# Sums of weight blocks moved from Pool to DVE, and joint DVE instructions, in the up projection of a hybrid decoder layer

## The reference, cut to what matters

```python
def conv_gated_mlp(h, w_up, ffn_conv, w_down):
    u = causal_dwconv(h @ w_up, ffn_conv)      # (1024, 1024) @ (1024, 5632), 3 taps along positions
    gate, up = jnp.split(u, 2, axis=-1)
    return (jax.nn.silu(gate) * up) @ w_down   # (1024, 2816) @ (2816, 1024)
```

## Time and profile before

| | |
|---|---|
| Median of 3 runs | 1482.48 us (1482.26 to 1483.81) |
| The profiled execution's own time | 1481.3 us |
| Its span in the profile | 1479.6 us |
| PE busy | 1433.3 us, 97% |
| DVE busy | 1056.7 us, 71% |
| ACT busy | 702.7 us, 47% |
| Pool busy | 367.9 us, 25% |
| Mean granted clock of TensorE | 0.993 |
| Pairs of the up projection | about 779 to 1130 us of the span |
| Down projection | about 1130 to 1352 us |

### The profile page before, as it was taken

How to read it: one execution, slowest core, us unless ns; L and a number is a source line. 1 busy time by engine, 2 the same in 40 slices (tenths; PEclk the granted TensorE clock), 3 DMA queues, 4 the chain that set the end, 5 groups by cost and what they waited for, 6 DMA issues and landing times.

```text
span 1479.6 us, 19630 instructions
## 1 busy us (share of the span) xinstructions
PE 1433.3 (97%) x7167; PEld 1199.8 (81%) x7167; DVE 1056.7 (71%) x1467; ACT 702.7 (47%) x1297; POOL 367.9 (25%) x314
## 2 busy tenths in 40 slices
PE   6999999999989999999999999999999999999996
PEld 5777888878879999888888887887788886888885
DVE  6666545551038888367897999999999599577566
ACT  5432456412326877357664443443345444454434
POOL 3000001100028677010013333332330387010010
PEclk9999999999998999999999999999999999999999
DMA  8653424545522332544442333334327755424232
GB/s 220 78 105 43 43 69 125 154 96 120 143 78 72 115 108 82 183 144 156 138 145 87 100 125 133 113 104 152 115 85 267 225 170 178 143 79 129 86 99 100
DMA packets 156318, 181.52 MB, mean 123 GB/s; under 512 B 21240, under 2 KB 96190, under 8 KB 156222
## 3 DMA queue, kind: packets, MB, share of 16 engines
q1 hardware_dynamic: 155968, 180.16, 42.4%
q10 hardware_dynamic: 254, 0.10, 0.0%
HBM read 130.95 MB, written 49.28 MB: 122 GB/s over the span
## 4 chain that ended last, share of the span: by engine, by line
PE 81%; DVE 13%; issue 2%; ACT 2%; DMA 1%; POOL 0%; SPq 0%; DVEq 0%; ACTq 0%; POOLq 0%
PE psum L2255 7%; PE psum L2257 7%; PE psum L2256 7%; PE psum L563 5%; PE psum L565 5%; PE psum L564 5%; PE psum L1202 5%; PE psum L2167 4%; PE psum L2169 4%; PE psum L2168 4%; PE psum L2194 3%; PE psum L2195 3%; PE psum L2196 3%; PE psum L1256 3%; PE psum L618 3%; PE psum L620 3%
## 5 line engine op out<-in xcount | busy, mean ns | idle before, releaser
L148 DVE TENSOR_TENSOR w_wlo<-w_raw,w_whi 128x1024 fp32r<-128x1024 f32 x70 | 93.8, 1340 | 253.8 <-ACT w_whi L142 253.7
L2255 PE MATMUL psum<-m_hi,w_whi 128*128 128x512 f32 x416 | 163.0, 392 | 7.1 <-DVE w_wlo L1821 6.3
L2257 PE MATMUL psum<-m_hi,w_wlo 128*128 128x512 f32 x416 | 162.0, 389 | 0.0
L2256 PE MATMUL psum<-m_lo,w_whi 128*128 128x512 f32 x416 | 161.9, 389 | 0.0
L142 ACT ACTIVATE w_whi<-w_raw 128x1024 fp32r<-128x1024 f32 x70 | 74.0, 1058 | 184.2 <-PE psum L2169 85.7
L563 PE MATMUL psum<-h_hi,w_whi 128*128 128x512 f32 x320 | 126.6, 396 | 3.1 <-DVE h_lo L834 3.1
L565 PE MATMUL psum<-h_hi,w_wlo 128*128 128x512 f32 x320 | 125.2, 391 | 0.0
L564 PE MATMUL psum<-h_lo,w_whi 128*128 128x512 f32 x320 | 125.1, 391 | 0.0
L2194 PE MATMUL psum<-w_whi,g_slot 128*128 128x512 f32 x308 | 122.3, 397 | 2.7 <-DVE w_wlo L2969 2.4
L2195 PE MATMUL psum<-w_wlo,g_slot 128*128 128x512 f32 x308 | 121.2, 394 | 0.0
L2196 PE MATMUL psum<-w_whi,g_slot 128*128 128x512 f32 x308 | 121.2, 393 | 0.0
(11 more groups left out here) (377 smaller groups left out, 3656.8 us busy)
## 6 DMA issues: line engine op xcount, KB each, us to landing
w_raw<-in_w_up SPq DMA_DIRECT2D x39, 512.0 KB, 4.0
w_raw<-in_w_in SPq DMA_DIRECT2D x36, 512.0 KB, 6.5
s_rows<-formed_sums SPq DMA_DIRECT2D x11, 1024.0 KB, 4.1
w_raw<-s_rows SPq DMA_DIRECT2D x44, 256.0 KB, 2.7
g_rows<-long_g SPq DMA_DIRECT2D x18, 512.0 KB, 2.7
w_raw<-g_rows SPq DMA_DIRECT2D x33, 256.0 KB, 3.1
w_raw<-in_w_out SPq DMA_DIRECT2D x16, 512.0 KB, 4.3
mixed_home<-in_w_down SPq DMA_DIRECT2D x32, 256.0 KB, 3.5
```

Of the source, the lines that this page charges most:

```text
L2255: pe.matmul(out, wh[:, part], hi(kt), start=(start and kt == 0), stop=False)
L2256: pe.matmul(out, wh[:, part], lo(kt), start=False, stop=False)
L2257: ins = pe.matmul(out, wl[:, part], hi(kt), start=False, stop=(stop and kt == KT // 2 - 1))
```

## The change

It has four parts.

- The 72 sums of the pairs go from Pool to DVE. Those of pair 0 stand between pieces of `dve_plain` (T1 behind piece 29, T2 behind the second tap of unit 6, T3 behind piece 30, T4 behind piece 33). In `dve_pairs`, T1 of pair c+1 stands behind remainder n+5, T2 behind n+6, T3 behind n+7 and T4 behind n+9. Pool has nothing to do in the pairs.
- The two results of T3 become one instruction over 1024 elements: the PSUM bank is read twice through a broadcast, and both outputs lie at one distance in a common buffer, `work`.
- NS2 and S3 of nine of the eleven formed sets (those from the pairs' own gated values) become one instruction, `e0` read twice, at the place of NS2.
- The down projection's Pool sums come in another order and behind other waits: the second group is split, so that B12's sums come last, and each group waits for the remainder of piece 14+i, 25+i, 36+i and 47+i.

For the joint instructions the buffers of the pairs lie in one tile. `copies[0]` now lies where `h_raws` was, so ACT waits once, in pair 0, for the last remainder taken from there (`sum_lo`); `short_acc` of the last plain unit lies in `formed`. A gap grows from 16 to 24 elements.

```diff
-        gap = s("home_gap", [P, 16])
+        gap = s("home_gap", [P, 24])
...
+                work = s("pair_work", [P, 8 * HALF + 6 * SEQ + 8], c=pairs)
+                line_at, form_at = 4 * HALF, 4 * HALF + 2 * SEQ + 8
+                g_at, acc_at = form_at + 4 * HALF, form_at + 4 * HALF + 2 * SEQ
...
+        def both(at, step):
+            return work[:, at:at + 2 * step].rearrange("p (b c) -> p b c", b=2)[:, :, 0:HALF]
+        u_early = line_at + self.PAD
+        self.copies_12, self.copy_3_and_line = both(HALF, HALF), both(3 * HALF, u_early - 3 * HALF)
+        self.forms_12, self.form_0_and_e1 = both(form_at + HALF, HALF), both(form_at, g_at + HALF - form_at)
...
     def made_count(self, m, i):
-        n = self.KH
-        return {2: i + 1, 4: n + 2 * i + 1, 5: n + 2 * i + 2, 6: 3 * n + i + 1}[m]
+        return {2: 0, 4: 1, 6: 2, 5: 3}[m] * self.KH + i + 1
...
             m.wait(act, key)
+            if c == 0:
+                act.wait_ge(s["sum_lo"], 2 * KT)
...
         if which in (self.NS2, self.S4):
             dve.wait_ge(s["formed"], 4 * use + (1 if which == self.NS2 else 3))
+        if i >= Units.PLAIN // 2 and which == self.S3:
+            return
+        if i >= Units.PLAIN // 2 and which == self.NS2:
+            twice = e0.unsqueeze(1).broadcast_to([P, 2, HALF])
+            dve.tensor_tensor(self.forms_12, twice, self.form_0_and_e1, ALU.subtract).then_inc(s["formed"], 2)
+            return
...
         piece(29)
+        units.sum(dve, 0, Units.T1, self.s["gated"])
         taps(6, 0)
+        units.sum(dve, 0, Units.T2)
         piece(30)
+        units.sum(dve, 0, Units.T3)
...
         piece(33)
+        units.sum(dve, 0, Units.T4)
         gate(6)
...
             units.remainder(dve, n + 5)
+            if c == 0:
+                for stored in (base - 2, base - 1):
+                    self.g_stored(dve, stored)
+            units.sum(dve, c + 1, Units.T1)
...
             units.remainder(dve, n + 6)
+            units.sum(dve, c + 1, Units.T2)
...
             self.dve_rest(dve, n + 7)
+            units.sum(dve, c + 1, Units.T3)
...
-            dve.tensor_tensor(self.long_line[1][:, early], of(p7), copy[2], ALU.add)
-            self.banks.release(dve.tensor_tensor(copy[3], of(p7), copy[1], ALU.add), p7)
+            twice = of(p7).unsqueeze(1).broadcast_to([P, 2, HALF])
+            self.banks.release(dve.tensor_tensor(self.copy_3_and_line, twice, self.copies_12, ALU.add), p7)
...
             self.dve_rest(dve, n + 9)
+            units.sum(dve, c + 1, Units.T4)
             self.dve_form(dve, c, self.S4)
...
     def pool(self, pool):
-        units = self.units
         for i in range(0, self.HT, 2):
             self.add(pool, "outp0", i)
-        units.sum(pool, 0, Units.T1, self.s["gated"])
-        units.sum(pool, 0, Units.T2)
-        units.sum(pool, 0, Units.T3)
-        units.sum(pool, 0, Units.T4)
-        for c in range(Units.PAIRS):
-            if c == 0:
-                for n in (2 * Units.PLAIN - 2, 2 * Units.PLAIN - 1):
-                    self.g_stored(pool, n)
-            for which in (Units.T1, Units.T2, Units.T3):
-                units.sum(pool, c + 1, which)
-            units.sum(pool, c + 1, Units.T4)
         self.pool_down(pool)
...
-        made, split = self.s["down_made"], lambda m, i: self.units.ready(pool, self.piece(m * self.KH + i))
+        made, left = self.s["down_made"], lambda u: self.units.ready(pool, self.piece(u))
...
-            split(0, i)
+            left(self.KH + self.AHEAD + i)
             pool.tensor_tensor(home(self.B11), home(self.B12), home(self.B11), ALU.subtract).then_inc(made, 1)
...
-            split(2, i)
+            left(2 * self.KH + self.AHEAD + i)
             pool.tensor_tensor(home(self.B11), home(self.B11), home(self.B22), ALU.subtract).then_inc(made, 1)
-            pool.tensor_tensor(home(self.B12), home(self.B22), home(self.B12), ALU.subtract).then_inc(made, 1)
...
-            split(1, i)
+            left(3 * self.KH + self.AHEAD + i)
             pool.tensor_tensor(home(self.B21), home(self.B21), home(self.B11), ALU.add).then_inc(made, 1)
+        for i in range(self.KH):
+            left(4 * self.KH + self.AHEAD + i)
+            pool.tensor_tensor(home(self.B12), home(self.B22), home(self.B12), ALU.subtract).then_inc(made, 1)
```

More of the change, by code:

```diff
@@ L1881, in __init__ @@
             with ExitStack() as pairs:
[L1882 to L1888, removed]
+                work = s("pair_work", [P, 8 * HALF + 6 * SEQ + 8], c=pairs)
+                line_at, form_at = 4 * HALF, 4 * HALF + 2 * SEQ + 8
+                g_at, acc_at = form_at + 4 * HALF, form_at + 4 * HALF + 2 * SEQ
+                self.copies = [work[:, i * HALF:(i + 1) * HALF] for i in range(4)]
+                long = lambda at, n: [work[:, at + u * n:at + (u + 1) * n] for u in range(2)]
+                self.long_line, self.long_g, self.long_acc = long(line_at, self.PAD + SEQ), long(g_at, SEQ), long(acc_at, SEQ)
+                self.long_line.reverse()
+                formed = work[:, form_at:g_at].rearrange("p (w c) -> p w c", w=4)
+        def both(at, step):
[3 more added lines that the diff above has]
+        self.forms_12, self.form_0_and_e1 = both(form_at + HALF, HALF), both(form_at, g_at + HALF - form_at)
+        odd, last = [sums[0][:, u, :] for u in range(2)], [formed[:, u, :] for u in range(2)]
         self.short_acc = [([self.acc[0][:], self.acc[1][:]], odd)[n % 2] for n in range(2 * Units.PLAIN - 1)] + [last]
         self.short_g = [sums[1][:, part, :] for part in range(2)]
-        self.formed, self.formed_all = [formed[:, i, :] for i in range(4)], formed[:]
+        self.formed, self.formed_all = [formed[:, i, :] for i in range(4)], formed
         with ExitStack() as ple:
@@ L2051, in store_g @@
         else:
-            i, src, part = n - Units.PLAIN, self.long_g[:, n % 2, :], slice(0, SEQ)
+            i, src, part = n - Units.PLAIN, self.long_g[n % 2], slice(0, SEQ)
         sp.dma_start(self.g_rows[i, :, part], src).then_inc(self.g_out[n % 2], 16)
@@ L2573, in act_down @@
             if u == 1:
-                self.act_smooth(act, 2 * Units.PLAIN + last, self.long_acc[0][:], self.FREED + 2 * (2 * Units.PLAIN + last + 1))
+                self.act_smooth(act, 2 * Units.PLAIN + last, self.long_acc[0], self.FREED + 2 * (2 * Units.PLAIN + last + 1))
             if product in (0, 2) and 0 <= t < self.HT:
@@ L2637, in act_pairs @@
                 self.banks.released(act, ("pair", c - 1, Units.B21))
-            self.banks.release(act.activation(self.copies[0][:], self.banks.of(key), ACT.Copy), key)
+            self.banks.release(act.activation(self.copies[0], self.banks.of(key), ACT.Copy), key)
             units.round(act, n + 4)
@@ L2645, in act_pairs @@
             else:
[L2646 removed]
+                self.act_smooth(act, base + c - 1, self.long_acc[0], self.FREED + 2 * (base + c))
             units.round(act, n + 6)
@@ L2655, in act_tap_up @@
         act.wait_ge(self.s["gated"], 2 * Units.PLAIN + c)
-        act.activation(self.long_acc[1][:], self.long_line[1][:, 0:SEQ], ACT.Copy,
+        act.activation(self.long_acc[1], self.long_line[1][:, 0:SEQ], ACT.Copy,
                        scale=self.first_tap(2 * Units.PLAIN + c, 1)).then_inc(self.s["tap0"], 1)
@@ L2662, in act_tap_gate @@
         act.wait_ge(self.s["gated"], 2 * Units.PLAIN + c)
-        act.activation(self.long_acc[0][:], self.long_line[0][:, 0:SEQ], ACT.Copy,
+        act.activation(self.long_acc[0], self.long_line[0][:, 0:SEQ], ACT.Copy,
                        scale=self.first_tap(2 * Units.PLAIN + c, 0)).then_inc(self.s["tap0"], 1)
@@ L2951, in dve_gate @@
         else:
-            out, acc, used = self.long_g[:, n % 2, :], [tile[:] for tile in self.long_acc], n >= 2 * Units.PLAIN + 2
+            out, acc, used = self.long_g[n % 2], self.long_acc, n >= 2 * Units.PLAIN + 2
         if used:
@@ L2981, in dve_form @@
         else:
-            e0, e1 = (self.long_g[:, 0, part] for part in (slice(0, HALF), slice(HALF, SEQ)))
-            o0, o1 = (self.long_g[:, 1, part] for part in (slice(0, HALF), slice(HALF, SEQ)))
+            e0, e1 = (self.long_g[0][:, part] for part in (slice(0, HALF), slice(HALF, SEQ)))
+            o0, o1 = (self.long_g[1][:, part] for part in (slice(0, HALF), slice(HALF, SEQ)))
             if which == self.S1:
@@ L3148, in dve_pairs @@
         late = slice(self.PAD + HALF, self.PAD + SEQ)
-        early = slice(self.PAD, self.PAD + HALF)
-        of, copy = self.banks.of, [tile[:] for tile in self.copies]
+        of, copy = self.banks.of, self.copies
         for c in range(Units.PAIRS):
@@ L3154, in dve_pairs @@
                 self.dve_join(dve, c - 1, Units.T4)
-                self.dve_taps(dve, last, 0, self.long_acc[1][:], self.long_line[1], 1)
+                self.dve_taps(dve, last, 0, self.long_acc[1], self.long_line[1], 1)
             units.remainder(dve, n + 3)
@@ L3190, in dve_join @@
```

(14 more changed lines are left out.)

6 lines of the change are left out of this document (3 added, 3 removed).

## The result

| | before | after |
|---|---|---|
| Median of the runs | 1482.37 us (1480.94 to 1483.81, 4 runs) | 1465.26 us (1464.80 to 1466.26, 4 runs) |
| Ratio to before, 95% interval | | 0.9885 (0.9868 to 0.9903) |
| Profiled execution, own time and span | 1481.3 and 1479.6 us | 1465.5 and 1463.7 us |

The account below looks back on a forecast made before the run. PE was taken to set the time, with DVE, slowed beside Pool's sums, holding it up. Winning 7.7 us in the pairs and 4.6 in the down projection took 1482.48 to 1470.2 us, range 1468 to 1477.

Parts of the forecast that it names:

- 7.7 us were counted as lost: Pairs: PE's 123 pieces took 342.3 us against 334.6 without stalls; all 7.7 us were counted as won.
- the new sums' slot 0.60: Pairs: each sum moved to DVE takes 0.60 us, eight in two pairs adding 4.8 us of DVE work.
- the joint instructions 1.13 against 1.14: Pairs: a joint instruction takes DVE 1.14 us like the gate, against 2 x 0.60; three save 0.2 us in two pairs.
- no wait for landed tiles: Pairs: T1's sum on DVE finds its two tiles landed, as SP issues them about a pair earlier; counted at 0.
- the idle place filled: Pairs: DVE's idle 0.5 us per pair, ahead of the remainder that waits for ACT's rounding, is likely filled by T1's sum.
- the 36.2 counted: Pairs: DVE's work for two pairs after the change with the idle place filled, 36.2 us against PE's 38.1.
- the stretch: Pairs: Pool's sums lengthen DVE's instructions with two SBUF inputs, by 6.3 us in two pairs, which the change removes.
- the slower rival: Pairs: the stretch has another cause than Pool, so added sums remove nothing; +41 us, 1523 us; chance 0.05 with waits included.
- 4.6 us were counted: Down projection: stalls of 4.3 us beside back-to-back Pool sums and a first one of 0.3, all won by spreading the sums.
- The new addresses I count at 0: Moved buffers: no effect on time, as the pieces read their hi and lo parts from where they did; 0 us.
- 94.7 us for 34 pieces as one pace of 2.78: Down projection before its stalled block: 2.78 us a piece with 0.3 of a first stall taken off, the base for counting stalls.
- The first rival: Pairs with formed sums: three to seven stalls remain, 2 to 7 us of the 12.3 stay, 1472.2 to 1477.2; chance 0.22.

Follow-up runs that it names:

- the extra work: The changed kernel with two more DVE sums of 480 elements in each pair, into an unused buffer: 1471.2 us, ratio 0.9926 to the kernel before.
- Experiment 4: The changed kernel with the 72 sums of the pairs back on Pool in their old places, joint instructions kept: 1472.5 us, ratio 0.9932 to the kernel before.
- experiments 4 and 5: The second of these: the changed kernel with the joint instructions taken apart again, sums on DVE: 1465.6 us, ratio 0.9885 to the kernel before.
- gap16_in_new: The changed kernel with only the gap ahead of the split slots back from 24 to 16 elements: 1471.1 us, ratio 0.9917 to the kernel before.
- gap24_in_old: The kernel before with only the gap grown from 16 to 24 elements: 1478.75 us, ratio 0.9977 to the kernel before.
- experiment 7: The changed kernel with two residual additions of the down projection's first output half moved from Pool to DVE: 1464.1 us, ratio 0.9883 to the kernel before.
- homes_shifted: The changed kernel with the weights' split homes 32 bytes further on and all other buffers 128: 1501.5 us, one run.

## Why the prediction was right and where it was wrong

*Right: what bounds the pairs, and what the change gives there.* 7.7 us were counted as lost and 7.6 came back. Each term held: the new sums' slot 0.60, the joint instructions 1.13 against 1.14, no wait for landed tiles, the idle place filled, DVE with 36.3 us of work in two pairs against the 36.2 counted, and the extra work bounds the room from above. Experiment 4 shows that the stretch was Pool's, so the slower rival falls; experiments 4 and 5 together show that the sums' move does it and the joint instructions don't. The Trainium skill's rule (SBUF — State Buffer, Who interferes with whom) that instructions with two SBUF inputs are held up by Pool and PSUM-fed ones aren't is borne out in kind: with the sums on Pool the formed sums have a mean of 1063 ns and the late half from PSUM 682.

*Right: the stalls of the down projection.* 4.6 us were counted, and at the old addresses (gap16_in_new) the stage went from 222.4 to 217.7, 4.7 less. That kernel is the one that the forecast describes, and its ratio of 0.9917 is 12.3 us, the forecast's own number. The account of the pairs and of the stalls was right by its mechanism. That the number came out to a tenth is luck, since the runs of one kernel spread by 1.5 us.

*Wrong: the step "The new addresses I count at 0".* Its reason, that the pieces read their parts from where they did, was untrue: g_slots 0, 2 and 3 lie behind the gap and moved by 32 bytes, and so did the operands of the embedding's matmuls. The slots are worth 4.1 us (gap16_in_new against the changed kernel, both at the new order) or 3.1 (gap24_in_old against before, where the stalled pieces hide some of it), the embedding 0.6 in both. With 4.7 in the place of 0 the sum gives 1465.5, where 1465.3 was measured. The range had no room for the term either: its lower end was made of a small stall and the spread of runs. It wasn't for want of rows. I took 94.7 us for 34 pieces as one pace of 2.78, when it is three pieces at 2.80 and one at 2.72. A mean over a stage hid what differed by slot, and that the pairs next to it ran at 2.72 asked for a reason.

*Missed, small:* the stall near the end of the down projection (at 1317.47 after) cost 0.4 us before and costs 0.9 after. PE now runs faster towards the place where Pool's residual addition holds DVE up. It was not in the sum; experiment 7 takes it away.

The first rival (some stalls stay) didn't happen, but was near: DVE is within 2.3 us in 38.1 of bringing them back. The interval of the measured ratio, 0.9868 to 0.9903, is 5.2 us wide in time, so differences of a few us are read here from the stages of the profiles and not from the whole times.

## What to carry to other kernels

Where Pool and DVE work side by side on SBUF tensors, count what Pool's work costs DVE: here eight Pool sums stretched DVE by 6.3 us (by the prediction's count of slots), and eight sums on DVE itself cost 4.8. The changed sizes and moved buffers of a diff are part of the change: list which operands of the bounding engine move, and compare their pace per piece before taking a mean over the stage. Where matmuls of one shape run at two paces in one trace, sort them by buffer first.

## What the runs showed of the hardware

- Twelve float32r matmuls of 128x128 by 512 took 2.72 us when the start addresses of the two SBUF operands' buffers differed by a multiple of 256 bytes, and 2.78 to 2.82 in the other cases tried (-32, +32, +64 and +128 bytes from such a multiple for the slots, 96 with the homes shifted). In a kernel with both kinds the matching pieces took 2.72 to 2.76. It is the relation of the two that counts: a shift of all buffers together by 32 bytes left the pairs at 334.7 us and the down projection at 213.7. Over this whole kernel it is worth 2.5% (homes_shifted, one run, 1501.5 us against 1465.3). Why the distance acts isn't settled by these runs, and whether other data types do the same wasn't tried.
- A DVE tensor_tensor that reads one PSUM bank twice through a broadcast and writes two distant SBUF regions had a slot of 1.13 us, where the gate, 1024 elements from SBUF alone, had 1.14 in the earlier trace rows.
